# A hybrid decoder step on one core: per-head sums of squares from a high and a low part instead of one fp32 product

## What is computed

```python
def rmsnorm(x, g):
    xf = x.astype(jnp.float32)
    r = lax.rsqrt(jnp.mean(xf * xf, axis=-1, keepdims=True) + EPS)
    return (xf * r).astype(x.dtype) * g
def project_qkv(h, w_qkv, q_norm, k_norm):
    p = (h @ w_qkv).reshape(b, t, N_GROUPS, 3, H_SLOT, HEAD_DIM)
    q = rmsnorm(p[:, :, :, 0], q_norm)
    k = rmsnorm(p[:, :, :, 1], k_norm)
    v = p[:, :, :, 2]
```

## Time and profile before

| what | value |
|---|---|
| median of 3 runs | 1394.62 us (1393.7 to 1395.48) |
| the profiled execution | 1394.49 us, of which the trace's span is 1392.9 us |
| PE busy | 1348.9 us (97%) |
| DVE busy | 727.9 us (52%) |
| ACT busy | 528.3 us (38%) |
| mean granted TensorE clock | 0.989 of 2.4 GHz |
| S_QKV and its tail | from about 603 us to about 985 us of the span |

### The profile page before, as it was taken

One profiled execution on the slowest core, in us unless ns is written; L12 is line 12 of the kernel. 1 busy time (PEld: TensorE's weight loads), 2 busy tenths in 40 slices (PEclk: granted clock), 3 DMA queues, 4 the chain that ended last, 5 costly groups with the idle time before them and its releaser, 6 DMA issues.

```text
span 1392.9 us, 27664 instructions
## 1 busy us (share of the span) xinstructions
PE 1348.9 (97%) x11153; PEld 1312.0 (94%) x11153; DVE 727.9 (52%) x1170; ACT 528.3 (38%) x839; POOL 21.2 (2%) x50
## 2 busy tenths in 40 slices
PE   6999999999999999999999899997999999999998
PEld 5999999999999999999889798886899999999998
DVE  4655466555555533344654545547665555553222
ACT  4322244333333322233554444545443333332121
POOL 0000000000000000000000000000000000000000
PEclk9999999999999999999999999999899999999999
DMA  6344435663454354544646426338134443445331
GB/s 174 92 152 152 151 110 161 209 175 106 130 167 152 104 166 135 161 133 150 176 125 199 140 84 190 120 119 261 31 106 149 152 150 105 151 149 161 100 94 62
DMA packets 256585, 195.16 MB, mean 140 GB/s; under 512 B 6581, under 2 KB 250789, under 8 KB 255362
## 3 DMA queue, kind: packets, MB, share of 16 engines
q1 hardware_dynamic: 253528, 139.17, 35.2%
q0 software_dynamic: 1792, 54.43, 10.8%
q10 hardware_dynamic: 1194, 0.54, 0.1%
HBM read 186.60 MB, written 65.21 MB: 181 GB/s over the span
## 4 chain that ended last, share of the span: by engine, by line
PE 91%; DVE 2%; SPq 2%; DMA 2%; issue 1%; ACT 1%; DVEq 0%
PE acc L1529 79%; PE acc L1557 2%; DMA skv<-new_rows 1%; PE N L1518 1%; PE N L1749 1%; SPq L516 1%; PE M L1701 1%; PE acc L1813 1%; PE M L1518 1%; PE acc L1518 1%; PE acc L1709 1%; DMA wraw<-in_sc_w_in_dram 1%; PE M L1813 1%; DVE wl L1030 1%; SPq L512 0%
## 5 line engine op out<-in xcount | busy, mean ns | idle before, releaser
L1529 PE MATMUL acc<-hh,wh 128*128 128x260 f32 x2288 | 468.6, 286 | 10.8 <-DVEq L1304 10.3
L1529 PE MATMUL acc<-hh,wl 128*128 128x260 f32 x2288 | 462.7, 284 | 0.0
L1529 PE MATMUL acc<-hl,wh 128*128 128x260 f32 x2288 | 461.8, 283 | 0.0
L715 ACT ACTIVATE wh<-wraw 128x1024 fp32r<-128x1024 f32 (+1 forms) x212 | 220.5, 1040 | 594.9 <-PE acc L1529 583.1
L1529 PEld LDWEIGHTS acc<-hh,wh 128*128 128x128 f32 x2288 | 355.0, 189 | 14.5 <-DVEq L1304 11.9
L1529 PEld LDWEIGHTS acc<-hh,wl 128*128 128x128 f32 x2288 | 354.2, 189 | 0.0
L1529 PEld LDWEIGHTS acc<-hl,wh 128*128 128x128 f32 x2288 | 353.6, 189 | 0.0
L1030 DVE TENSOR_TENSOR wl<-wraw,wh 128x1024 fp32r<-128x1024 f32 (+1 forms) x212 | 254.2, 1199 | 173.7 <-ACT wh L715 170.9
L1529 PE MATMUL acc<-yh,wh 128*128 128x260 f32 x848 | 173.1, 285 | 5.2 <-DVE x L1440 5.2
L1529 PE MATMUL acc<-yh,wl 128*128 128x260 f32 x848 | 171.2, 283 | 0.0
L1529 PE MATMUL acc<-yl,wh 128*128 128x260 f32 x848 | 171.0, 283 | 0.0
(11 more groups left out here) (218 smaller groups left out, 1108.6 us busy)
## 6 DMA issues: line engine op xcount, KB each, us to landing
out_dram<-in_cache_kv_d_dram POOLq DMA_DIRECT2D x24, 1364.0 KB, 6.3
wraw<-in_ffn_w_gate_dram SPq DMA_DIRECT2D x44, 512.0 KB, 3.9
wraw<-in_ffn_w_up_dram SPq DMA_DIRECT2D x44, 512.0 KB, 3.9
wraw<-in_attn_w_qkv_dram SPq DMA_DIRECT2D x36, 512.0 KB, 4.2
out_dram<-in_cache_kv_d_dram POOLq DMA_DIRECT2D x8, 2044.0 KB, 8.6
wraw<-in_ffn_w_down_dram SPq DMA_DIRECT2D x32, 448.0 KB, 3.8
wraw<-in_sc_w_in_dram SPq DMA_DIRECT2D x24, 512.0 KB, 3.9
wraw<-in_ffn_w_down_dram SPq DMA_DIRECT2D x16, 512.0 KB, 4.0
```

What stands on the lines that cost most here:

```text
L715: nc.scalar.activation(wh[c % 2][:, 0:k], wraw[:, c % 4, 0:k], ACT.Copy).then_inc(hi_done, 1)
L1529: ins = T.matmul(acc[:, par, h2, 0:HALF], w[c % 2][:, k, :], a[:, k0 + k, h2, :], start=(first and k == 0 and n == 0), stop=(last and k == ...
```

## The change

The squares are made as before in fp32 (`sq`), then ACT rounds them to fp32r (`sq_hi`), DVE writes the rest, `sq - sq_hi`, in fp32r (`sq_lo`), and PE adds up two fp32r matmuls per half against `head_r`, the rounded copy of `head_ones`, which holds 1/64 exactly. So `head_sums` is four fp32r matmuls in place of two fp32 ones. `sq_hi` lies over `y32` and `sq_lo` over `ssq`. Hence `hots` and `rbs` move to `newh` and `hist_ffn`, SP waits for another semaphore before it loads `hots`, and `ssq` is cleared again at the end of the stage. The buffers are single: ACT's `squares` of tile q now waits until PE has summed tile q-1. In ACT's order, `squares` goes ahead of the exponentials at steps 1 and 7 and between them at step 5 (blocks 1 to 3); at steps 2 and 8 it stays behind `head_rms`. On DVE, `squares_lo` stands behind the units' reciprocals and ahead of `normalise`.

```diff
@@ squares, ACT
                 act.wait_ge(qk_ready, q + 1)
-                nc.scalar.activation(sq, qk_t[:, q % 2, :].rearrange("p (h n) -> p h n", h=2),
-                                     ACT.Square).then_inc(qsq_ready, 1)
+                if q:
+                    act.wait_ge(qms_ready, q)
+                ch.after(nc.scalar.activation(sq, qk_t[:, q % 2, :].rearrange("p (h n) -> p h n", h=2), ACT.Square))
+                nc.scalar.activation(sq_hi, sq, ACT.Copy).then_inc(qsq_hi, 1)
@@ the steps, ACT
+                q = 6 * p + 2 * (c // 3) + c % 3 - 1
+                if c in (1, 4, 7):
+                    squares(q)
                 if p and c % 2:
                     exp_unit(n, 0)
+                    if c == 5:
+                        squares(q)
                     exp_unit(n, 1)
                     scale_unit(n)
                 if c in SUMS and p >= SUMS[c][0]:
                     head_rms(6 * (p - SUMS[c][0]) + SUMS[c][1])
-                if c % 3:
-                    squares(6 * p + 2 * (c // 3) + c % 3 - 1)
+                if c in (2, 8) or c == 5 and not p:
+                    squares(q)
@@ once, DVE
+            dve.wait_ge(pool_set, 6)
+            V.tensor_copy(head_r[:], head_ones[:])
@@ DVE
+            def squares_lo(q):
+
+                dve.wait_ge(qsq_hi, q + 1)
+                V.tensor_tensor(sq_lo, sq, sq_hi.bitcast(F32), ALU.subtract).then_inc(qsq_ready, 1)
@@ the steps, DVE
                     unit_inv(n)
+                if c % 3:
+                    squares_lo(6 * p + 2 * (c // 3) + c % 3 - 1)
@@ behind the last chunk, DVE
             unit_o(n0 - 1, B1)
+            dve.wait_ge(qms_ready, 6 * NP_)
+            V.memset(ssq[:], 0.0)
             normalise(p, 5)
@@ head_sums, PE
-                    ins = T.matmul(N[:, h2, 0:HALF], head_ones[:], sq[:, h2, :], start=True, stop=True)
+                    T.matmul(N[:, h2, 0:HALF], head_r[:], sq_hi[:, h2, :], start=True, stop=False)
+                    ins = T.matmul(N[:, h2, 0:HALF], head_r[:], sq_lo[:, h2, :], start=False, stop=True)
@@ SP, step 1 of block 0
-                    sp.wait_ge(yl_ready, DK + FK)
+                    sp.wait_ge(rows_t, 2)
```

More of the change, by code:

```diff
@@ L168, in build @@
         r = sb("r", [P, 2, HALF])
+        with ExitStack() as same:
+            sq_lo = same.enter_context(nc.sbuf_tensor("sq_lo", [P, 2, HALF], F32R))[:]
         ssq = sb("ssq", [P, 2, HALF])
@@ L176, in build @@
         sq = sv[:, 0:2 * HALF].rearrange("p (h n) -> p h n", h=2)
+        with ExitStack() as same:
+            sq_hi = same.enter_context(nc.sbuf_tensor("sq_hi", [P, 2, HALF], F32R))[:]
         y32 = sb("y32", [P, 2, HALF])
@@ L186, in build @@
         head_ones = sb("head_ones", [P, P])
+        head_r = sb("head_r", [P, P], F32R)
         gq = sb("gq", [P, 2])
@@ L276, in build @@
         qk_ready = sem("qk_ready")
+        qsq_hi = sem("qsq_hi")
         qsq_ready = sem("qsq_ready")
@@ L366, in build @@
         se, pts = cv[0:W, 0:NSC], cv[:, NSC:NSC + NG * W].rearrange("p (g m) -> p g m", g=NG)
-        hots = y32[0:NB].rearrange("p h n -> p (h n)")[:, 0:NSC + 2]
-        rbs = newh[0:NB, 0:NG * NP_ * W].rearrange("p (g q b h) -> p g q b h", g=NG, q=NP_, b=NS)
+        hots = newh[0:NB, 0:NSC + 2]
+        rbs = hist_ffn[0:NB, 0].rearrange("p x f -> p (x f)")[:, 0:NG * NP_ * W] \
+            .rearrange("p (g q b h) -> p g q b h", g=NG, q=NP_, b=NS)
         B0, B1 = acc[:, 1, 0], acc[:, 1, 1]
```

## The result

| what | before | after |
|---|---|---|
| median | 1395.05 us (1393.70 to 1395.93, 4 runs) | 1414.58 us (1405.14 to 1420.03, 4 runs) |
| ratio | | 1.0134, 95% interval 1.0075 to 1.0192 |
| profiled execution (span) | 1394.49 us (1392.9) | 1411.7 us (1410.1) |
| mean granted TensorE clock | 0.989 | 0.971 |

The four runs of after lie in the order of their clocks: 1420.03 and 1417.45 us at 0.965, 1411.70 us, the profiled one, at 0.971, and 1405.14 us at 0.977.

A forecast was written before the change was run, and what follows sets the result against it. The prediction took PE, busy 97% of the span, to bound the kernel. Its sum was 1394.5 - 5.6 (saving) + 4.8 (wait at step 8) + 12.4 (clock) = 1406.1 us, with an 8-in-10 range of 1391.5 to 1419 us.

The forecast's parts named there:

- the side that had 0.73: Whole kernel: the outcome slower than before, given a chance of 0.73, against same 0.18 and faster 0.09.
- the 1406.1 of the sum: Whole kernel: forecast time in us, from the old time, the saving, the wait at step 8 and the clock.
- The saving: PE's sums of squares: 0.48 us each in place of 0.88, so 5.6 us less on the path.
- The count of 14 on the path: Sums that shorten the path by 0.40 us each, in block 0, steps 5, 6 and 0, and behind the last chunk.
- The list of hidden ones: Sums forecast to save 0: step 0 of block 1, steps 2 and 3 of blocks 1 to 3.
- DVE's and ACT's new work elsewhere: Extra copies and low parts outside step 8: forecast to cost 0, or 0.3 us a block at step 5 if not.
- The wait at step 8: Blocks 1 to 3: late `sample_pts` makes PE stand about 2.0 us, net 1.6 us each, 4.8 us in all.
- The clock: Behind the stands at step 8: two of three expected to lose full clock, 6.2 us each, +12.4 us.
- my 11 us for a clock that doesn't come back: Cost of a fall if the clock stays low past step 0's values and sum, doubling its alternating stretch too.
- rival 3: All three step-8 stands lose the clock, or two for the longer stretch: 1412 to 1427 us; chance 0.25.
- The DMA waits: Steps 2 and 3 of blocks 1 to 3: PE arrives 0.8 us sooner, waits 0.8 us longer, end unchanged.
- A short stand: Rival at step 8: stand much shorter than thought, 17 sums save 6.8 us, 1387.7 us; chance 0.08.

The follow-up runs named there:

- experiment 10: Kernel before with only the nine key and value output transfers moved from step 1 to step 5: 1382.17 us, 0.9919 of the kernel before.
- experiment 1: Changed kernel with DVE's two `sample_pts` copies moved ahead of `squares_lo` and `normalise` at step 8 of blocks 1 to 3: 1388.7 us, 0.9957 of the kernel before.
- experiment 7: experiment 1 plus an SP wait holding the group-2 key cache load until the group-1 query rows have landed: 1383.35 us, 0.9927 of the kernel before.
- experiment 4: Changed kernel with PE running 16 throw-away 260-column matmuls before its wait at step 8 of blocks 1 to 3: 1390.58 us, 0.9972 of the kernel before.
- experiment 5: Kernel before with two chained clears of `ssq` on DVE ahead of `sample_pts` at step 8 of blocks 1 to 3: 1407.42 us, 1.008.
- experiment 6: Kernel before with fourteen chained clears on DVE ahead of the readout at steps 2, 5 and 8 of block 0: 1401.44 us, 1.0047.
- experiment 2: Kernel before with four chained clears of `ssq` on DVE ahead of `sample_pts` at step 8 of blocks 1 to 3: 1419.09 us, 1.0182.

## Why the prediction was right, and where it was not

The time is inside the range, on the side that had 0.73, and some 8.5 us over the 1406.1 of the sum. The path is the forecast one, a stand at step 8 and the clock behind it. That the total came so near has some luck in it, as the clock cost 8.5 us more than forecast and the DMA waits 3.0 us less.

- **The saving.** 0.88 to 0.48 us a sum, steps of block 0 from 6.65 to 6.25: as forecast. The count of 14 on the path held too, steps 5 and 6 giving 0.79 us in block 1. The list of hidden ones was right for step 3 and step 0 of block 1, and experiment 10 shows that it is not the DMA alone that hides step 3's.
- **DVE's and ACT's new work elsewhere** costs nothing that can be seen. In block 1 of after, step 4 is 1.59 us longer (9.50 in place of 7.91), as DVE comes late to its readout, and steps 5 and 6 are shorter by more than that; the three sum to 26.65 us in place of 27.44, which is the 0.40 us of two sums. In experiment 1 it is the same, and step 8 is 0.41 shorter.
- **The wait at step 8.** Forecast: `normalise` at 827.09, `sample_pts` done at 828.46, 2.0 us of standing, +4.8 in all. Measured: 827.66, 828.98, 1.76 to 1.88 us, +4.3. The mechanism is as described, and experiment 1 removes it.
- **The clock** is the term that was mis-sized. I had two falls of 6.2 us, 12.4. There were three, of 6.5, 5.0 and 9.4 us, 20.9. The price was near for two of them, and the third came nearer to my 11 us for a clock that doesn't come back; the count was one short. The profiled execution is my rival 3, at the edge of its times, and two more runs (1417 and 1420 us) lie in it, as does the median; the one of 1405.14 us, at the highest clock of the four, may be a case with fewer falls, which no trace shows.
- **The DMA waits** were forecast as unchanged in their end. They came 3.0 us shorter together, so this step failed. In block 1 `key_sums` is queued behind `squares_lo`, so the load that it releases goes out later and disturbs the query rows less; experiment 7 bears this out in the other blocks, by the same wait put in on purpose. In block 2 the nine transfers ahead on SP took 1.1 us less, and in block 3 the rows took longer to land; why, no run shows. This hid a part of the loss.
- **The rivals.** A short stand was to give 17 x 0.40 = 6.8 us and 1387.7 us. Experiment 1 makes just that case and gives 1388.7.

What stays open: what the chip weighs when it takes the clock away. Experiments 1 and 4 show that the mixed stretch keeps the clock when no idle time is ahead of it, and experiment 5, with the 1.60 us that held, that the length of the stand alone doesn't decide. Idle time isn't needed everywhere either: before lost the clock behind 2.68 us of two-column matmuls in a row and 0.98 us of transposes, with PE busy. What the work behind a stand adds is not shown, as experiment 6 made a single long stand and that one lost the clock as well. Nor was it tried why the clock stayed low for 28 us in block 3 and 24 us in experiment 5, and came back after 10 to 14 elsewhere.

## What to carry to other kernels

An operation that becomes cheaper on the bounding engine can still cost time by the order in which its helpers are queued: look who stands behind the new wait on the helper engine, and put what PE needs next ahead of it. Price every new stand of PE twice, by its length and by the clock behind it. Here the second was the larger where small matmuls followed (20.9 against 4.3 us), and the smaller in the one case with full products behind it (1.5 against 2.9 us). Throw-away matmuls in the gap can pay, as in experiment 4. A wait for a DMA gives back or takes away small gains of other edits, so cut it first, here by issuing what nobody waits for later.

## What the runs showed of the hardware

- Stands ahead of mixed work, half of it two-column matmuls, lost the full clock in three of three cases at 1.76 to 1.88 us (after), three of three at 2.29 to 2.42 us (experiment 2) and one of three at 0.96 to 1.08 us (experiment 5). The single stand of 2.88 us ahead of full products lost it too (experiment 6).
- The lower level lasted for 10 and 14 us behind two stands of after, 28 us behind the third and 24 us in experiment 5, with PE busy through most of it, but less than 5 us behind the stand in full work.
- Sixteen matmuls of 260 columns (2.07 us) in place of the idle time kept the clock at 1.00 through the mixed stretch of step 8 (experiment 4).
- A transfer of 512 KB landed 1.8 us later (6.57 against 4.78 us) with a load of 256 KB issued 1.5 us behind it instead of 3.6.
